# First attention of a two-block model kernel: reciprocal sums applied to the exponentials on GpSimd instead of to the head outputs

## The chip, the cores and the metric

One Trainium2 chip, one of its cores. The metric is the device time of one execution in microseconds (us). The engines named here: TensorE (PE) multiplies, PEld is its weight load; VectorE (DVE), ScalarE (ACT) and GpSimd (POOL) do the elementwise work; SyncE (SP) starts transfers. Each engine runs its own instructions in program order and waits on semaphores for the others.

## What is computed

The whole kernel is two transformer-like blocks of depth two, on 512 tokens of width 1024. The part that the change touches is the first attention (`mla_mix` in the first layer): twelve heads of 64, causal, 512 queries and 512 keys in blocks of 128.

```python
s = jnp.einsum('bhqd,bhkd->bhqk', qb, k) * scale
p = masked_softmax(s, key_pos[None, :] <= tq[:, None]).astype(v.dtype)
return jnp.einsum('bhqk,bhkd->bqhd', p, v)
# masked_softmax: e = exp(s - max) * mask;  e / max(sum(e), 1e-30)
```

After it come four heads of attention over 256 memory tokens (`memory_attention`), then the product with `w_out`, a layer norm, a feed-forward part, and so on.

## The kernel before

All work is written out by hand, engine by engine, and ordered by semaphores; nothing is scheduled by a tool. The twelve heads are the units u = 0 to 11 and are handled in six pairs i = 0 to 5. The four memory heads are the units 12 to 15. Two buffers of everything exist, and unit u uses buffer u % 2.

A unit goes through these steps, with the name of the helper and the engine:

1. `project_q` on TensorE: the query projection of one head, two matmuls of 512 columns into bank 3 of PSUM. `take_q` (ScalarE) and `rotate_q` (VectorE, three instructions) bring it to SBUF as QT.
2. `scores` on TensorE: four matmuls, one for each block of 128 queries, over 512, 384, 128 and 256 keys (the tiles in `STILES`), together 1280 columns.
3. `soft_max` on VectorE: adds the mask, takes the maximum, writes the masked scores to PR[:, s] in SBUF and the maximum to NB.
4. `softmax_exp` on ScalarE: the exponential in place in PR[:, s], and its row sums in SM[:, s]. It signals `p_ready`.
5. `own_sums` on VectorE: RS = 1/SM, 128x4. It signals `rs_ready`.
6. `probs_t` on TensorE: ten 128x128 transposes of PR[:, s]. `probs_out` on ScalarE and on VectorE copy the result to PT.
7. `pv_pair` (called by `mla_pv`) on TensorE: the product with the values for the two heads of a pair at once, transposed, so that features lie on the partitions and tokens on the columns.

The transposed probabilities are not normalised. `factors` on TensorE therefore multiplies the identity by RS spread over 64 columns, for both heads and four blocks of queries: eight small products that put 1/sum of every token on the 64 rows of each head. ScalarE copies the result to FR (`factors_out`, signal `factor_sb`), and VectorE multiplies the head outputs by it (`pair_out`, signal `o_done`).

TensorE's order inside `mla_pair(i)` is: transposes of unit 2i, projection of 2i+3, scores of 2i+2, transposes of 2i+1, scores of 2i+3, factors, projection of 2i+4, product with the values of pair i. The projection writes the same PSUM bank 3 as the factors before it, so it waits for `factor_sb`.

VectorE's order inside `mla_pair(i)` is: `pair_out` of pair i-1, `own_sums(2i)`, the copy of the transposes of 2i, `rotate_q(2i+3)`, `soft_max(2i+2)`, `own_sums(2i+1)`, the copy of the transposes of 2i+1, `soft_max(2i+3)`, `rotate_q(2i+4)`. Pair 4 has one projection only, and pair 5 none: the first two memory heads' scores stand in their place.

GpSimd has little in this stage: when ScalarE has rounded a chunk of the output to XH (`o_high`), it subtracts to get the rest, XL (`o_low`), one instruction of 128x512 for each of eight chunks. The memory heads keep the factors, before and after.

## Time and profile before

| | us |
|---|---|
| median of 3 runs | 2621.22 (2612.64 to 2634.3) |
| profiled execution | 2629.39 |
| its span | 2627.6 |
| PE busy in it | 2530.0 (96%) |
| DVE busy | 1454.3 (55%) |
| ACT busy | 961.7 (37%) |
| POOL busy | 1070.0 (41%) |
| first attention, twelve heads | from about 498 to 588 us of the span |

The busy figures count every instruction's duration. Matmuls overlap each other, and the gap between the starts of two groups tells more than a duration does. The clock granted to TensorE is 1.2 or 2.4 GHz and is printed as 0.50 or 1.00. In the page's 40 slices of the span it reads 9 tenths or more everywhere but in one slice, which reads 7.

### The profile page before, as it was taken

To read this page: it belongs to the slowest core of one execution; us is meant where nothing else is said; L and a number is where in the kernel's file an instruction comes from. 1 tells how busy PE (TensorE), PEld (TensorE's weight loads), DVE (VectorE), ACT (ScalarE), POOL (GpSimd) and SP (SyncE) were. 2 spreads that over 40 slices of the span, in tenths; PEclk is the share of its full clock that TensorE was granted. 3 is DMA by queue.
4 is the path that set the end of the run, shared out by engine and by line. 5 is a ranking of instruction groups with operands and counts; after the bars stand their busy time and mean duration, and the time that the engine had idled before them with its cause. 6 is when DMAs were issued, how large, how long until landed. Compare 5 with 4: busy or idle time off the path is not lost.

```text
span 2627.6 us, 34202 instructions
## 1 busy us (share of the span) xinstructions
PE 2530.0 (96%) x12558; PEld 2039.6 (78%) x12558; DVE 1454.3 (55%) x2060; ACT 961.7 (37%) x1500; POOL 1070.0 (41%) x712
## 2 busy tenths in 40 slices
PE   8999999899999999999999999889999998989998
PEld 7888887556788887888888777678888877777886
DVE  6545446664755646354654658564333354797653
ACT  4222225453522224232212578553222233353332
POOL 3978866003749834033633402273012054022401
PEclk9999999999999999799999999999999988999999
DMA  8354446211444463244442321235333235334231
GB/s 205 96 141 137 122 120 158 57 27 50 127 128 136 149 156 105 66 137 126 141 146 86 84 72 47 73 111 153 118 106 105 88 97 155 134 119 125 84 93 64
DMA packets 439113, 292.04 MB, mean 111 GB/s; under 512 B 34355, under 2 KB 420202, under 8 KB 435530
## 3 DMA queue, kind: packets, MB, share of 16 engines
q1 hardware_dynamic: 422042, 212.38, 28.6%
q0 software_dynamic: 16944, 77.93, 9.6%
q8 instruction: 83, 1.36, 0.2%
q14 instruction: 44, 0.36, 0.0%
HBM read 272.50 MB, written 20.92 MB: 112 GB/s over the span
## 4 chain that ended last, share of the span: by engine, by line
PE 83%; DVE 6%; POOL 5%; ACT 3%; issue 2%; DMA 1%; DVEq 0%; SPq 0%; ACTq 0%; POOLq 0%
PE ps L766 38%; PE ps L771 19%; PE ps L848 5%; PE ps L875 4%; PE ps L1055 2%; PE ps L1043 1%; DVE wl L2237 1%; POOL SW L3063 1%; POOL NS L3061 1%; PE ps L1458 1%; PE ps L1070 1%; PE ps L1416 1%; POOL NS L3060 1%; PE ps L1229 1%; PE ps L1195 1%
## 5 line engine op out<-in xcount | busy, mean ns | idle before, releaser
L2237 DVE TENSOR_TENSOR wl<-raw,wh 128x1024 fp32r<-128x1024 f32 x376 | 619.4, 1648 | 884.1 <-ACT wh L1681 880.9
L1681 ACT ACTIVATE wh<-raw 128x1024 fp32r<-128x1024 f32 x385 | 408.2, 1061 | 1329.4 <-PE ps L771 1160.4
L766 PE MATMUL ps<-XH,wh 128*128 128x512 f32 x1832 | 720.0, 393 | 0.5 <-ACT wh L1681 0.5
L766 PE MATMUL ps<-XL,wh 128*128 128x512 f32 x1832 | 713.9, 390 | 0.0
L771 PE MATMUL ps<-XH,wl 128*128 128x512 f32 x1832 | 453.2, 389 | 0.0
L766 PEld LDWEIGHTS ps<-XH,wh 128*128 128x128 f32 x1832 | 344.5, 188 | 77.1 <-issue 4.9
L766 PEld LDWEIGHTS ps<-XL,wh 128*128 128x128 f32 x1832 | 344.5, 188 | 73.1 <-issue 2.2
L771 PEld LDWEIGHTS ps<-XH,wl 128*128 128x128 f32 x1832 | 343.8, 188 | 71.7 <-issue 0.4
L766 PE MATMUL ps<-HH,wh 128*128 128x512 f32 x528 | 207.1, 392 | 0.0
L766 PE MATMUL ps<-HL,wh 128*128 128x512 f32 x528 | 205.5, 389 | 0.0
L3174 POOL TENSOR_TENSOR NS<-AW,CS 128x2048 f32<-128x2048 f32 x32 | 116.7, 3648 | 215.5 <-PE ps L1143 206.7
L771 PE MATMUL ps<-HH,wl 128*128 128x512 f32 x528 | 132.9, 391 | 0.9 <-DVE wl L2237 0.8
L771 PEld LDWEIGHTS ps<-HH,wl 128*128 128x128 f32 x528 | 98.9, 188 | 23.1 <-DVE wl L2237 2.0
L766 PEld LDWEIGHTS ps<-HL,wh 128*128 128x128 f32 x528 | 99.1, 188 | 21.5 <-issue 1.0
L766 PEld LDWEIGHTS ps<-HH,wh 128*128 128x128 f32 x528 | 99.1, 188 | 21.5 <-issue 1.0
L3011 POOL COPY ACC<-XT 128x512 f32<-128x512 f32 x6 | 3.7, 613 | 258.2 <-DVE XT L2302 258.2
L3175 POOL TENSOR_TENSOR NS<-NS 128x1024 f32<-128x1024 f32 x32 | 102.7, 3209 | 2.5
L3248 POOL DMA_DIRECT2D BS<-s_b x12 | 6.6, 559 | 227.3 <-PE ps L1195 181.3
L848 PE MATMUL ps<-XH,wh 128*128 128x512 f32 x172 | 77.5, 451 | 20.1 <-ACT XH L1766 10.3
L2257 DVE TENSOR_TENSOR HL<-HF,HH 128x512 f32 (+1 forms) x88 | 89.0, 1012 | 10.5
L1861 ACT ACTIVATE PR<-PR,NB 128x512 f32<-128x512 f32 (+3 forms) x144 | 79.0, 551 | 22.0 <-DVE NB L2520 21.3
L3155 POOL TENSOR_TENSOR XL<-O,XH 128x512 fp32r<-128x512 f32 x16 | 20.4, 1276 | 155.7 <-ACT XH L1894 155.7
(522 smaller groups left out, 4079.0 us busy)
## 6 DMA issues: line engine op xcount, KB each, us to landing
raw<-in_ffn_w_gu SPq DMA_DIRECT2D x176, 512.0 KB, 3.8
raw<-in_ffn_w_down SPq DMA_DIRECT2D x64, 512.0 KB, 3.7
AW<-in_ada_w POOLq DMA_DIRECT2D x24, 1024.0 KB, 7.5
raw<-in_ffn_w_down SPq DMA_DIRECT2D x32, 384.0 KB, 3.2
BS<-s_b POOLq DMA_DIRECT2D x12, 1024.0 KB, 6.1
raw<-in_odd_w_in SPq DMA_DIRECT2D x24, 512.0 KB, 3.8
raw<-in_even_w_in SPq DMA_DIRECT2D x22, 512.0 KB, 4.4
s_w<-SW POOLq DMA_DIRECT2D x12, 512.0 KB, 6.4
```

The lines of the kernel that those rows point to most:

```text
L766: pe.matmul(ps[:, p % 4, 0:n], wh[:, p % 2, k * P:(k + 1) * P], x[:, k, 0:n], start=k == 0 and x is hi, stop=False)
L771: mm = pe.matmul(ps[:, p % 4, 0:n], wl[:, p % 2, k * P:(k + 1) * P], hi[:, k, 0:n], start=False, stop=k == nk - 1)
L848: return pe.matmul(ps[:, (p + e) % 4, 0:n], w[:, (p + e) % 2, c * P:(c + 1) * P], x[:, c, 0:n], start=c == 0 and w is wh and x is hi, stop ...
L875: return pe.matmul(ps[:, (p + e) % 4, :], w[:, (p + e) % 2, k * P:(k + 1) * P], x[:, k, :], start=k == 0 and w is wh and x is HH, stop=k = ...
L1043: mm = pe.transpose(ps[:, bank, col:col + P], PR[:, s, POFF[q] + kb * P:POFF[q] + (kb + 1) * P], IDENT[:])
L1055: mm = pe.matmul(ps[e * HD:(e + 1) * HD, 7, kb * P:T], vals(kb, e), PT[:, e, at:at + T - kb * P], start=kb == 0, stop=kb == TT - 1)
L1681: act.activation(wh[:, p % 2, :], raw[:, p % 4, :], ACT.Copy).then_inc(w_hi, 1)
L1861: ins = act.activation(PR[:, s, POFF[t]:POFF[t] + (t + 1) * P], PR[:, s, POFF[t]:POFF[t] + (t + 1) * P], ACT.Exp, bias=NB[:, s, t:t + 1], ...
L2237: dve.tensor_tensor(wl[:, p % 2, :], raw[:, p % 4, :], wh[:, p % 2, :].bitcast(F32), ALU.subtract).then_inc(w_lo, 1)
L2257: dve.tensor_tensor(HL[:, k, :], HF[:, f:f + 1, :], HH[:, k, :].bitcast(F32), ALU.subtract).then_inc(h_ready, 1)
L3174: step(pool.tensor_tensor(prod, AW[:, n % 2], CS[:, :, e:e + 1].broadcast_to([P, KD, 2 * P]), ALU.mult))
L3175: step(pool.tensor_tensor(prod[:, 0:4], prod[:, 0:4], prod[:, 4:8], ALU.add))
```

## The change

Between the reciprocal and the transposes GpSimd now multiplies the exponentials in place by the reciprocal sums: `scale_probs`, four instructions for each of the twelve units, over 512, 384, 128 and 256 columns, with RS broadcast along the columns. The last of them signals `p_scaled`, and in the first layer `probs_t` waits for that in place of `p_ready`.

The factors of the six pairs go: `mla_factors` on TensorE, `factors_out` on ScalarE. `pair_out` becomes `plain_out` for them, a copy out of PSUM, at the same place in VectorE's order. `project_q` waits for `factor_sb` no more. `o_low` of chunk c stands behind the scaling of unit 2c+4 for c = 0 to 3. The counts of the later factors are lower by six (`PLAIN`), and the rotated key's semaphore is merged into `kv_ps`, which frees one semaphore.

```diff
@@ -423,7 +423,7 @@
         ln_aff = sem("ln_aff")
         mla_in_s = sem("mla_in_s")
         scaled = sem("scaled")
-        kr_ps = sem("kr_ps")
+        p_scaled = sem("p_scaled")
         kr_rot = sem("kr_rot")
         kr_keys = sem("kr_keys")
         x_read = sem("x_read")
...
@@ -570,6 +570,7 @@
 
             return 16 * (p // 4 + 1) + 32 * sum(q <= p and q % 4 == p % 4 for q in range(BASE["wo1"], BASE["wo1"] + COUNT["wo1"]))
 
+        PLAIN = HEADS // 2
         PAIR = {"mla": 0, "mem0": 6, "mem1": 8, "nsa": 10}
         S_WAIT = (1, 3, 3, 4)
         MEM_BANK = ((4, 2, 4, 2), (4, 6, 6, 4))
...
@@ -1036,7 +1037,10 @@
 
             def probs_t(u, s):
 
-                pe.wait_ge(p_ready, u + 1)
+                if mem_layer[0] == 0:
+                    pe.wait_ge(p_scaled, u + 1)
+                else:
+                    pe.wait_ge(p_ready, u + 1)
                 wait(pe, pt_act, 2 * u)
                 wait(pe, pt_dve, u)
                 for n, (bank, col, q, kb) in enumerate(TBLOCKS):
...
@@ -1107,7 +1111,7 @@
                                        start=m == 0, stop=m == MT - 1)
                 mm.then_inc(pv_ps, 1)
                 pe.wait_ge(rs_ready, u + 2)
-                pe.wait_ge(factor_sb, n)
+                wait(pe, factor_sb, n - PLAIN)
                 factors(MEM_PV[mem_layer[0]][h // 2][1], RS)
 
             def s5_fill(t):
...
@@ -1309,7 +1313,7 @@
                     pe.wait_ge(mla_in_s, 80)
                     pe.wait_ge(*taken_at("mla", 3))
                     pe.wait_ge(vm_ready, 4)
-                    pe.matmul(ps[ROPE:2 * ROPE, 6, :], PERM[:], KR, start=True, stop=True).then_inc(kr_ps, 1)
+                    pe.matmul(ps[ROPE:2 * ROPE, 6, :], PERM[:], KR, start=True, stop=True).then_inc(kv_ps, 1)
 
             panels("mla", 6, split_at("mla"), after=mla_squares)
             def project_q(h, s, turn):
...
@@ -1317,7 +1321,6 @@
                 pe.wait_ge(sp_in[s], 48 * turn + 48)
                 wait(pe, q_nope, h)
                 wait(pe, q_rot, 2 * h)
-                wait(pe, factor_sb, turn - 1)
                 for k in range(2):
                     mm = pe.matmul(ps[:, 3, :], WQ[:, s, k, :], CQ[:, k, :], start=k == 0, stop=k == 1)
                 mm.then_inc(q_ps, 1)
...
@@ -1363,17 +1366,9 @@
                 mla_scores(2 * i + 2, 0)
                 probs_t(2 * i + 1, 1)
                 mla_scores(2 * i + 3, 1)
-                mla_factors(i, 2 * i + 4)
                 if more > 1:
                     project_q(2 * i + 4, 0, i + 2)
                 mla_pv(i)
-
-            def mla_factors(i, projected, bank=3):
-
-                pe.wait_ge(rs_ready, 2 * i + 2)
-                pe.wait_ge(q_nope, projected)
-                pe.wait_ge(q_rot, 2 * projected)
-                factors(bank, RS)
 
             def mla_pv(i):
 
...
@@ -1385,7 +1380,6 @@
             probs_t(10, 0)
             mem_scores(12, 0)
             probs_t(11, 1)
-            mla_factors(5, 12, 6)
             mla_pv(5)
             mem_scores(13, 1)
             for h in range(MEM_HEADS):
...
@@ -1884,7 +1878,7 @@
 
             def factors_out(n, bank=3):
 
-                act.wait_ge(factor_ps, n + 1)
+                act.wait_ge(factor_ps, n + 1 - PLAIN)
                 wait(act, o_done, n)
                 act.activation(FR, ps[:, bank, :], ACT.Copy).then_inc(factor_sb, 1)
 
...
@@ -1949,7 +1943,7 @@
             take_q(0, 0)
             for g in range(14):
                 if g < 6:
-                    act.wait_ge(kv_ps, g + 1)
+                    act.wait_ge(kv_ps, g + 2)
                     act.activation(KT[0:HD, 2 * g, :], ps[0:HD, 4 + g % 4, :], ACT.Copy).then_inc(kv_act, 1)
                     if g == 5:
                         take_q(1, 1)
...
@@ -1957,7 +1951,7 @@
                         act.wait_ge(kr_rot, 2)
                         act.activation(KT[HD:QK, 0:6, :], KR2[:, 0:1, :].broadcast_to([ROPE, 6, T]), ACT.Copy).then_inc(kr_keys, 1)
                 elif g % 2 == 0:
-                    act.wait_ge(kv_ps, g + 1)
+                    act.wait_ge(kv_ps, g + 2)
                     act.activation(V[:, (g - 6) // 2, 0:6 * HD], ps[:, 4 + g % 4, 0:6 * HD], ACT.Copy).then_inc(kv_act, 1)
 
             take_q(2, 0)
...
@@ -1973,7 +1967,6 @@
                     take_q(2 * i + 3, 1)
                 softmax_exp(2 * i + 2, 0)
                 probs_out(2 * i + 1, 1)
-                factors_out(i)
                 softmax_exp(2 * i + 3, 1)
                 if more > 1:
                     take_q(2 * i + 4, 0)
...
@@ -1986,8 +1979,6 @@
                 probs_out(10 + h, h)
                 if h == 0:
                     o_high(4, (o_done, 5))
-                else:
-                    factors_out(5, 6)
                 mem_exp(12 + h, h, h)
             for h in range(MEM_HEADS):
                 u = 12 + h
...
@@ -2531,9 +2522,14 @@
 
             def pair_out(n, dst, bank=7):
 
-                dve.wait_ge(factor_sb, n + 1)
+                dve.wait_ge(factor_sb, n + 1 - PLAIN)
                 dve.wait_ge(pv_ps, n + 1)
                 dve.tensor_tensor(dst, ps[:, bank:bank + 1, :], FR.rearrange("p (o t) -> p o t", o=1), ALU.mult).then_inc(o_done, 1)
+
+            def plain_out(i):
+
+                dve.wait_ge(pv_ps, i + 1)
+                dve.tensor_copy(O[:, i, :], ps[:, 7, :]).then_inc(o_done, 1)
 
             def mem_max(u, n, s):
                 bank = MEM_BANK[n // 4][n % 4]
...
@@ -2619,7 +2615,7 @@
                 dve.tensor_tensor(QT[HD:QK, s, :], RT[HD:QK, 0, :], RT[HD:QK, 1, :], ALU.add).then_inc(q_rope, 1)
 
 
-            dve.wait_ge(kr_ps, 1)
+            dve.wait_ge(kv_ps, 1)
             dve.wait_ge(mla_in_s, 80)
             dve.tensor_tensor(KR2[:, 0, :], ps[ROPE:2 * ROPE, 6, :], ROT[ROPE:2 * ROPE, :], ALU.mult).then_inc(kr_rot, 1)
             dve.tensor_tensor(KR2[:, 1, :], KR, ROT[0:ROPE, :], ALU.mult).then_inc(dve_link, 1)
...
@@ -2628,14 +2624,14 @@
             rotate_q(0, 0)
             for g in range(14):
                 if g < 6:
-                    dve.wait_ge(kv_ps, g + 1)
+                    dve.wait_ge(kv_ps, g + 2)
                     dve.tensor_copy(KT[0:HD, 2 * g + 1, :], ps[HD:P, 4 + g % 4, :]).then_inc(kv_dve, 1)
                     if g == 5:
                         rotate_q(1, 1)
                         dve.wait_ge(kr_rot, 2)
                         dve.tensor_copy(KT[HD:QK, 6:12, :], KR2[:, 0:1, :].broadcast_to([ROPE, 6, T])).then_inc(kr_keys, 1)
                 elif g % 2:
-                    dve.wait_ge(kv_ps, g + 1)
+                    dve.wait_ge(kv_ps, g + 2)
                     dve.tensor_copy(V[:, (g - 6) // 2, 6 * HD:], ps[:, 4 + g % 4, 0:6 * HD]).then_inc(kv_dve, 1)
 
             def o_chunk(c):
...
@@ -2648,7 +2644,7 @@
             def mla_pair(i, more=2):
 
                 if not (isinstance(i, int) and i == 0):
-                    pair_out(i - 1, o_chunk(i - 1))
+                    plain_out(i - 1)
                 own_sums(2 * i, 0)
                 probs_out(2 * i, 0)
                 if more > 0:
...
@@ -2666,14 +2662,14 @@
             for h in range(2):
                 u = 10 + h
                 if h == 0:
-                    pair_out(4, o_chunk(4))
+                    plain_out(4)
                 own_sums(u, h)
                 probs_out(u, h)
                 mem_max(u + 2, h, h)
             for h in range(MEM_HEADS):
                 u = 12 + h
                 if h == 0:
-                    pair_out(5, o_chunk(5))
+                    plain_out(5)
                 if h == 2:
                     pair_out(6, o_chunk(6))
                 own_sums(u, u % 2)
...
@@ -3154,7 +3150,18 @@
                 pool.wait_ge(mix_hi, n + c + 1)
                 pool.tensor_tensor(XL[:, c, :], O[:, c, :], XH[:, c, :].bitcast(F32), ALU.subtract).then_inc(x_split, 1)
 
-            for c in range(KD):
+            def scale_probs(u, s):
+
+                pool.wait_ge(rs_ready, u + 1)
+                for t, bank, col in STILES:
+                    pr = PR[:, s, POFF[t]:POFF[t] + (t + 1) * P]
+                    ins = pool.tensor_tensor(pr, pr, RS[:, s, t:t + 1].broadcast_to([P, (t + 1) * P]), ALU.mult)
+                ins.then_inc(p_scaled, 1)
+            for u in range(HEADS):
+                scale_probs(u, u % 2)
+                if u >= 4 and u % 2 == 0:
+                    o_low(0, u // 2 - 2)
+            for c in range(HEADS // 2 - 2, KD):
                 o_low(0, c)
             norm("wo0")
 
```

The hunks left out only subtract `PLAIN` from a count of the memory heads and the second attention.

The order on TensorE in pair 1 of the twelve heads, before (PR are the exponentials, RS the reciprocal sums, CQ and WQ the query projection, KT and QT keys and queries, PT and V the transposed probabilities and the values):

```order
L1043 MATMUL ps<-IDENT,PR 128x128 [waits pt_dve,pt_act,p_ready]
L1043 MATMUL ps<-IDENT,PR 128x128 x9
L1070 MATMUL ps<-KT,QT 128x512 [waits s_sb,q_rope,q_nope]
L1070 MATMUL ps<-KT,QT 128x384 [waits s_sb]
L1070 MATMUL ps<-KT,QT 128x128 [waits s_sb]
L1070 MATMUL ps<-KT,QT 128x256 [waits s_sb]
L1062 MATMUL ps<-IDENT,RS 64x128 [waits q_rot,q_nope,rs_ready]
L1062 MATMUL ps<-IDENT,RS 64x128 x7
L1322 MATMUL ps<-CQ,WQ 128x512 [waits q_rot,factor_sb,q_nope,sp_in0]
L1322 MATMUL ps<-CQ,WQ 128x512
L1055 MATMUL ps<-PT,V 64x512 [waits o_done,pt_dve,pt_act]
```

and the same place of the change:

```order
L1047 MATMUL ps<-IDENT,PR 128x128 [waits pt_dve,pt_act,p_scaled]
L1047 MATMUL ps<-IDENT,PR 128x128 x9
L1074 MATMUL ps<-KT,QT 128x512 [waits s_sb,q_rope,q_nope]
L1074 MATMUL ps<-KT,QT 128x384 [waits s_sb]
L1074 MATMUL ps<-KT,QT 128x128 [waits s_sb]
L1074 MATMUL ps<-KT,QT 128x256 [waits s_sb]
L1325 MATMUL ps<-CQ,WQ 128x512 [waits q_rot,q_nope,sp_in0]
L1325 MATMUL ps<-CQ,WQ 128x512
L1059 MATMUL ps<-PT,V 64x512 [waits o_done,pt_dve,pt_act]
```

The eight products with RS are gone, the projection has lost the wait for `factor_sb`, and the transposes wait for `p_scaled`.

VectorE at the turn from one pair to the next, in the change (O is the head output, the copy stands where the multiplication by FR stood, so the order is that of before):

```order
L2610 TENSOR_TENSOR RT<-ps,ROT 32x512 [waits q_rope,q_ps]
L2611 TENSOR_TENSOR RT<-ps,ROT 32x512
L2615 TENSOR_TENSOR QT<-RT 32x512 [waits s_ps,q_rot]
L2532 COPY O<-ps 128x512 [waits pv_ps]
L2521 RECIPROCAL RS<-SM 128x4 [waits p_ready]
L2516 COPY PT<-ps 128x512 [waits t_ps]
```

The reciprocal of the first unit of a pair stays behind the copy that waits for the product of the pair before (`pv_ps`), and now the scaling and the transposes hang on that reciprocal.

GpSimd in the change, around the fifth unit:

```order
L3158 TENSOR_TENSOR PR<-PR,RS 128x512 [waits rs_ready]
L3158 TENSOR_TENSOR PR<-PR,RS 128x384
L3158 TENSOR_TENSOR PR<-PR,RS 128x128
L3158 TENSOR_TENSOR PR<-PR,RS 128x256
L3151 TENSOR_TENSOR XL<-O,XH 128x512 [waits mix_hi]
L3158 TENSOR_TENSOR PR<-PR,RS 128x512 [waits rs_ready]
```

Before, only the eight rows `XL<-O,XH` stood here.

## Rows read from the trace of the kernel before

**Rows 1.** The page's first part: busy time, share of span, instructions.
```profile
PE 2530.0 (96%) x12558; PEld 2039.6 (78%) x12558; DVE 1454.3 (55%) x2060; ACT 961.7 (37%) x1500; POOL 1070.0 (41%) x712
```
**Rows 2.** Busy time in a stretch; granted clock (PEclk), DMA share, GB/s last.
```profile
542.00:554.00 12.00, 11.21 (x72) 7.05 (x71) 8.41 (x27) 6.98 (x22) 0.00 (x0) 1.00 0.13 22
```
**Rows 3.** Timeline, TensorE in pair 2: start, us, engine, line, tiles, [idle before].
```profile
538.28 1.31 PE L1043 MATMUL ps<-IDENT,PR 128*128 128x128 f32 x10
541.15 2.32 PE L1070 MATMUL ps<-KT,QT 96*128 96x512 f32 x8
543.10 1.23 PEld L1043 LDWEIGHTS ps<-IDENT,PR 128*128 128x128 f32 x10
544.40 2.36 PE L1070 MATMUL ps<-KT,QT 96*128 96x512 f32 x8
546.69 1.09 PE L1062 MATMUL ps<-IDENT,RS 128*64 128x128 f32 x16
548.57 1.96 PE L1322 MATMUL ps<-CQ,WQ 128*128 128x512 f32 x4 [0.79 <-ACT NS L1889]
550.46 2.37 PE L1055 MATMUL ps<-PT,V 128*64 128x512 f32 x16
552.76 1.31 PE L1043 MATMUL ps<-IDENT,PR 128*128 128x128 f32 x10
```
**Rows 4.** Timeline, VectorE in the same pair 2.
```profile
538.47 0.69 DVE L2536 TENSOR_TENSOR O<-ps,NS 128x512 f32<-128x512 f32 x1 [0.25 <-PE ps L1055]
539.08 0.17 DVE L2530 RECIPROCAL RS<-SM 128x4 f32<-128x4 f32 x1
...
542.80 0.69 DVE L2619 TENSOR_TENSOR QT<-RT 32x512 f32<-32x512 f32 x1
...
543.52 0.69 DVE L2520 CUSTOM_DVE_ANT_0 PR<-ps,CAUS 128x512 f32<-128x512 f32 x1
...
545.16 0.17 DVE L2530 RECIPROCAL RS<-SM 128x4 f32<-128x4 f32 x1
```
**Rows 5.** GpSimd instructions by form: duration in ns min/median/max, first and last start.
```profile
L3174 POOL TENSOR_TENSOR NS<-AW,CS x32: 3603/3615/4652, 681.9 to 1390.3; 128x2048 f32<-128x2048 f32 x32
L3155 POOL TENSOR_TENSOR XL<-O,XH x16: 1262/1270/1296, 526.1 to 1684.2; 128x512 fp32r<-128x512 f32 x16
L3212 POOL TENSOR_TENSOR SC<-SC,CMASK x6: 727/736/739, 1574.9 to 1669.3; 128x256 f32<-128x256 f32 x6
```
**Rows 6.** Timeline, VectorE and GpSimd instructions that overlap, in a layer norm.
```profile
636.65 1.67 DVE L2237 TENSOR_TENSOR wl<-raw,wh 128x1024 fp32r<-128x1024 f32 x1 [0.47 <-ACT wh L1681]
637.20 2.28 POOL L3021 TENSOR_TENSOR NS<-NS 128x512 f32<-128x512 f32 x1
```
**Rows 7.** Timeline, first, fifth and last pair.
```profile
509.48 0.17 DVE L2530 RECIPROCAL RS<-SM 128x4 f32<-128x4 f32 x1
523.80 1.31 PE L1043 MATMUL ps<-IDENT,PR 128*128 128x128 f32 x10
567.24 1.31 PE L1043 MATMUL ps<-IDENT,PR 128*128 128x128 f32 x10
578.82 1.31 PE L1043 MATMUL ps<-IDENT,PR 128*128 128x128 f32 x10
581.98 1.07 PEld L1043 LDWEIGHTS ps<-IDENT,PR 128*128 128x128 f32 x10 [0.33 <-issue]
582.96 0.17 DVE L2530 RECIPROCAL RS<-SM 128x4 f32<-128x4 f32 x1
585.84 2.37 PE L1055 MATMUL ps<-PT,V 128*64 128x512 f32 x16 [1.52 <-ACT PT L1869]
588.14 1.99 PE L1086 MATMUL ps<-KM,QM 64*128 64x256 f32 x8
```
**Rows 8.** Two matmul groups behind idle stretches, and granted clock near the first.
```profile
505.47 3.62 PE L1070 MATMUL ps<-KT,QT 96*128 96x512 f32 x8 [3.05 <-DVE NB L2520]
507.00:508.00 1.00, 1.00 (x4) 0.70 (x3) 0.30 (x2) 1.00 (x5) 0.00 (x0) 0.50 0.00 0
```

More of the change, by code:

```diff
@@ L1082, in mem_scores @@
                 if h == 3 and layer == 1:
-                    pe.wait_ge(factor_sb, PAIR["mem1"] + 1)
+                    pe.wait_ge(factor_sb, PAIR["mem1"] + 1 - PLAIN)
                     pe.wait_ge(o_done, PAIR["mem1"] + 1)
@@ L1472, in nsa_factors @@
                 else:
-                    pe.wait_ge(factor_sb, PAIR["nsa"] + 2 * j + 1)
+                    pe.wait_ge(factor_sb, PAIR["nsa"] + 2 * j + 1 - PLAIN)
                 factors(bank, W4)
@@ L1483, in cmp_t @@
                 pe.wait_ge(c_p, j + 1)
-                pe.wait_ge(factor_sb, PAIR["nsa"] + 2 * j + 2)
+                pe.wait_ge(factor_sb, PAIR["nsa"] + 2 * j + 2 - PLAIN)
                 for t in range(TT):
@@ L1497, in _ @@
             pe.wait_ge(qs_ready, 2)
-            pe.wait_ge(factor_sb, PAIR["nsa"])
+            pe.wait_ge(factor_sb, PAIR["nsa"] - PLAIN)
             nsa_scores(20, 0, 0)
```

## Prediction

> **What bounds the kernel now.** I read the page's busy shares first: TensorE is busy 96% of the span and VectorE 55% [rows 1]. That is a mean over stages, so next the stretch of the first attention: in 12 us of pair 2 TensorE is busy 11.21 us at the full granted clock, GpSimd 0 us [rows 2]. The stage runs at TensorE's pace. The timeline then shows the cadence [rows 3]: the transposes of pair 2 start at 538.28, those of pair 3 at 552.76, so a pair takes 14.48 us, and each group starts where the one before ends, with one exception: the factors (L1062) start at 546.69 and the projection behind them only at 548.57, having waited for ScalarE's copy of the factors. These 1.88 us are factors plus wait. What the reader is to see besides is where the reciprocals stand [rows 4]. TensorE's transposes show no idle time before them, so the exponentials are there in time. But the reciprocals are late: the first of a pair runs at 539.08, after TensorE has begun the transposes of the same unit, and the second at 545.16, again after the transposes of its unit (543.10). Before the change nobody is hurt by that, since only the factors at 546.69 need them.
>
> **What the change removes.** The factors and the wait for their copy: 1.88 us in each of the pairs 0 to 3 [rows 3]. In pair 4 no projection follows, so only the products go, which I take as 0.9 (a duration of 1.09 that overlaps its neighbour). In pair 5 the factors lie under a wait: the product with the values waits another 1.52 us for ScalarE's copy of the transposes [rows 7]. ScalarE loses six copies, which are off the path. VectorE's multiplication becomes a copy of the same 128x512 from PSUM; I cost that at nothing; if it were 0.1 us off, six times that is below a microsecond.
>
> **What it adds: the price of one scaling, P.** Four GpSimd instructions over 512, 384, 128 and 256 columns. No row has just this form. From above: subtractions with two full inputs take 1.270 us for 512 and 0.736 us for 256 columns [rows 5], so 2.09 ns a column and 0.20 us fixed; that gives 1.27, 1.00, 0.47 and 0.74, together 3.48 us. From below: the multiplication by an operand broadcast along the columns takes 3.615 us for 2048 columns [rows 5], 1.77 ns each, which with nothing for four starts is 2.26 us for 1280. The operation is that of the second row, the sizes are those of the first. So I take 0.20 us for each start and (3.615 - 0.20)/2048 = 1.67 ns a column: 0.8 + 2.1 = 2.9, rounded to P = 3.0 us. The range keeps 2.26 and 3.48.
>
> **Where it lies.** Not beside anything. Take TensorE's first transposes of a pair in the old trace as T0 = 538.28.
> - First unit. VectorE's copy of the old pair's output stands ahead of the reciprocal and waits for TensorE's last product, so the reciprocal ends at 539.25, 0.97 us after T0 [rows 4]. GpSimd starts about 0.08 later, takes P, and TensorE hears of it about 0.09 later (hops like those between other engines here, an estimate). New start T1 = T0 + 0.97 + 0.17 + 3.0 = T0 + 4.14. Queued behind on TensorE: everything, in order.
> - Second unit. Its reciprocal stands behind the rotation and the soft_max of the next first unit, and these need the projection and scores that follow T1. In the old trace it ends at 545.33, T0 + 7.05: the rotation ends at 543.49, the soft_max starts at 543.52, and the reciprocal follows its last tile [rows 4]. All of it moves with T1. New start of the second transposes T2 = T1 + 7.05 + 0.17 + 3.0 = T1 + 10.22; in the old trace it was T0 + 4.82 (543.10).
> - From there TensorE runs through: 552.76 - 543.10 = 9.66 less 1.88 is 7.78 us [rows 3].
>
> A pair of the middle takes 4.14 + 10.22 + 7.78 = 22.14 us instead of 14.48: +7.66, three times +22.98. Pair 0: the first reciprocal ends at 509.65 [rows 7], transposes at 512.82, the next pair at 512.82 + 10.22 + 7.78 = 530.82 instead of 523.80: +7.02. Pair 4 takes 11.58 (567.24 to 578.82); its tail behind the second transposes is 11.58 - 4.82 - 0.9 = 5.86, so 4.14 + 10.22 + 5.86 = 20.22: +8.64. Pair 5: the second reciprocal ends at 583.13, 4.31 behind the first transposes (it has a memory head's maximum ahead of it instead of a soft_max); its transposes start 4.31 + 0.17 + 3.0 = 7.48 behind T1. The old tail 581.98 to 588.14 is 6.16, and less the 1.52 of waiting 4.64 [rows 7]. So 4.14 + 7.48 + 4.64 = 16.26 instead of 9.32: +6.94. **Sum: 7.02 + 22.98 + 8.64 + 6.94 = +45.6 us.** P is in it twelve times, so 2.26 gives +36.7 and 3.48 gives +51.4.
>
> `o_low` on GpSimd, moved into the stage, is 1.27 us behind a first unit's scaling [rows 5], while the second scaling comes 7.1 us after it: hidden. Were it not, it would cost at most 1.27 four times. Behind the stage TensorE goes straight on; no wait there could absorb the shift.
>
> **Does VectorE slow GpSimd down?** In the layer norm a GpSimd addition of 512 columns takes 2.28 us beside a VectorE subtraction that started first [rows 6], against 1.27 for a similar one alone. Here VectorE's instructions read PSUM, except the last of the rotation (0.69 us, ends at 543.49), and while GpSimd scales, VectorE waits for the very transposes that wait for GpSimd. So I add nothing. The Trainium skill (SBUF — State Buffer, the passage on the shared port pair) says that a VectorE instruction with two SBUF inputs contends with a GpSimd instruction that reads SBUF, and one with at most one doesn't. By that rule nothing is added either, and the slow row agrees with it. The skill's GPSIMD Engine Reference, section 4.1, advises against two-input elementwise work on GpSimd, about twice VectorE's time; by its 4497 ns for 2048 columns the scaling is an estimated 2.8 us, and the sum would be 2 us lower. The trace's subtractions are somewhat dearer.
>
> **What the stalls do to the clock.** TensorE will idle twice a pair, 4.1 us and 10.22 - 4.82 = 5.4 us, twelve stalls. Where it sat idle 3.05 us in the old trace, the scores behind took 3.62 us instead of 2.36, and the granted clock read 0.50, which is 1.2 of 2.4 GHz [rows 3, 8]. I expect that behind nearly every stall. If the first two groups behind a stall, some 3.3 us at the full clock [rows 3], go 3.62/2.36 = 1.53 times slower, a stall costs 1.7 us, and all of it is on the path, since these groups feed the next reciprocal or the next pair: 12 x 1.7 = +20 us. Ends: nothing, and 3 us a stall, +36. The Trainium skill (TensorE: Matmul & The Clock Gate, Part 1) says that idling drops the clock to half and sustained work restores it; the trace agrees, by the 0.50 behind the idle 3.05 us.
>
> **Total** 45.6 + 20 = +66 us. Against the profiled execution, 2629.4, that is 2695; it stands 8 us above the median of the runs, so by the median 2621.2 + 66 = **2687 us**, 2.5% slower.
>
> **The rivals.**
> - The clock stays up, or falls only now and then: +37 to +51, 2658 to 2673. For it: through a whole stage with TensorE 93% busy it holds. Against: the idle stretches are longer than the one that lost it. Chance 0.22.
> - The clock falls and stays low over most of the stage, or GpSimd takes 5 us a scaling (2.28 us for 512 columns as in [rows 6] would give 1280 x 4.45 ns = 5.7): +100 or more, above 2720. Against the first: dense groups follow every stall. Against the second: VectorE is waiting then. Chance 0.10.
> - The other side: the scaling is hidden and TensorE only loses the factors: 4 x 1.88 + 0.9 = -8.4 us, 2613. The mechanism would need the reciprocals one group of work earlier. They stand behind the previous product and behind the next soft_max [rows 4], and the order of VectorE is unchanged, so I give it 0.02. For the stage to cost under 1% (26 us), P would have to be below 3.0 - (45.6 - 26)/12 = 1.4 us even with the clock up, and no row of GpSimd is that fast: 0.03.
> - That the change doesn't do what it says is excluded by the order: `probs_t` waits for `p_scaled`.
>
> **How the numbers follow.** The forecast has 0.63. The range is from the clock staying up with the cheapest scaling, +37, less some scatter of the runs, to the dearest scaling with 3 us a stall, 51.4 + 36 = +87, plus scatter: 2655 to 2718. A difference under 1% can't be told from none here. Slower by over 1%: 0.63 + 0.22 + 0.10 = 0.95; within 1%: 0.04; faster: 0.01.
>
> **What the new profile would show.** Pairs of the stage 22 to 26 us apart instead of 14.48; before each group of transposes TensorE idle, released by GpSimd's PR; the four scalings together 2.3 to 3.5 us; the reciprocal 1 us behind the last product; the granted clock at 0.50 in parts of the stage; no wait for the copy of the factors. The sum is wrong if transposes start before the reciprocal's copy is done, if the scalings are much longer or shorter, or if time appears outside 508 to 600 us.

## The result and the profile after

The changed kernel takes 2684.98 us (median of 4 runs, 2677.88 to 2697.75) against 2618.08 us for the kernel before (4 runs, 2612.64 to 2634.3): 66.9 us more, a ratio of 1.0253 with a 95% interval of 1.0213 to 1.0292. The forecast was 2687 us. (The ratios and intervals of this document are estimated from all runs of a kernel and of the kernel before, and differ a little from the quotient of two medians.)

The page of the changed kernel, its busy time and two of its groups (line, engine, tiles, count | busy us, mean ns | idle before, and what ended it):

```profile
span 2696.0 us, 34023 instructions
PE 2552.4 (95%) x12462; PEld 2053.2 (76%) x12462; DVE 1457.8 (54%) x2060; ACT 960.7 (36%) x1494; POOL 1103.0 (41%) x760
L1047 PE MATMUL ps<-IDENT,PR 128*128 128x128 f32 x360 | 58.4, 321 | 51.4 <-POOL PR L3158 50.2
L3158 POOL TENSOR_TENSOR PR<-PR,RS 128x512 f32<-128x512 f32 (+3 forms) x48 | 33.0, 717 | 154.8 <-DVE RS L2521 154.8
```

The span has grown by 68.4 us. TensorE's busy time has grown by 22.4 of them (2552.4 against 2530.0 us, [rows 1]) although it executes 96 matmuls fewer, which already points at a lower clock; the other 46.0 are idle time. The third line tells where most of that lies: ahead of the transposes TensorE sat idle 50.2 us in all, released by GpSimd. GpSimd's 48 instructions are busy for 33.0 us, so the stalls are longer than the scaling itself.

TensorE's timeline over two pairs of the middle (start, us, engine, line, tiles, [idle before <- what ended it]):

```profile
539.20 2.40 PE L1047 MATMUL ps<-IDENT,PR 128*128 128x128 f32 x10 [3.83 <-POOL PR L3158]
541.39 3.36 PE L1325 MATMUL ps<-CQ,WQ 128*128 128x512 f32 x4
544.58 2.32 PE L1074 MATMUL ps<-KT,QT 96*128 96x512 f32 x8
551.65 2.39 PE L1047 MATMUL ps<-IDENT,PR 128*128 128x128 f32 x10 [4.75 <-POOL PR L3158]
553.84 2.70 PE L1074 MATMUL ps<-KT,QT 96*128 96x512 f32 x8
556.38 1.88 PE L1325 MATMUL ps<-CQ,WQ 128*128 128x512 f32 x4
558.19 2.38 PE L1059 MATMUL ps<-PT,V 128*64 128x512 f32 x16
564.40 2.02 PE L1047 MATMUL ps<-IDENT,PR 128*128 128x128 f32 x10 [3.83 <-POOL PR L3158]
...
590.22 2.39 PE L1047 MATMUL ps<-IDENT,PR 128*128 128x128 f32 x10 [3.83 <-POOL PR L3158]
```

These answer [rows 3]. Pairs start 25.2 and 25.8 us apart instead of 14.48. There is one stall ahead of each group of transposes, 3.83 us for the first unit and 4.75 us for the second, and behind each stall the transposes take 2.0 to 2.4 us, where they took 1.31.

VectorE and GpSimd in the same stretch, which answer [rows 4]:

```profile
548.60 0.17 DVE L2521 RECIPROCAL RS<-SM 128x4 f32<-128x4 f32 x1
548.85 2.75 POOL L3158 TENSOR_TENSOR PR<-PR,RS 128x512 f32<-128x512 f32 x4 [9.71 <-DVE RS L2521]
...
560.62 0.69 DVE L2532 COPY O<-ps 128x512 f32<-128x512 f32 x1 [0.18 <-PE ps L1059]
561.34 0.18 DVE L2521 RECIPROCAL RS<-SM 128x4 f32<-128x4 f32 x1
561.60 2.75 POOL L3158 TENSOR_TENSOR PR<-PR,RS 128x512 f32<-128x512 f32 x4 [9.99 <-DVE RS L2521]
564.31 1.26 POOL L3151 TENSOR_TENSOR XL<-O,XH 128x512 fp32r<-128x512 f32 x1
```

The chain is seen link by link: the product of the pair ends, VectorE copies it, takes the reciprocal, GpSimd scales for 2.75 us, TensorE transposes. GpSimd had been idle almost 10 us before each of these two scalings. The moved `o_low` (L3151) runs behind the scaling and delays nobody.

The windows of the changed kernel (behind the five busy times stand PEclk, the DMA share and GB/s), first from unit 1's scores to the first product with `w_out`, then about one pair:

```profile
506.00:681.00 175.00, 118.28 (x451) 72.13 (x452) 62.78 (x172) 59.11 (x177) 41.67 (x55) 0.77 0.05 12
542.00:567.00 25.00, 16.42 (x61) 9.67 (x60) 10.03 (x27) 8.39 (x25) 6.73 (x9) 0.84 0.06 11
```

The clock is 0.77 on average over the stage and 0.84 over that pair, where a stretch of the middle had 1.00 before [rows 2]. (The page of the kernel before has two slices of the clock at 8 besides the one at 7; all three lie behind this stage.)

For the experiments two lengths are read from each timeline: the heads' part, from the scores of unit 1 (505.47 in [rows 8]) to the product with the values of pair 5 (585.84 in [rows 7]), and the whole stage, on to the first product with `w_out`:

```profile
506.15 3.96 PE L1074 MATMUL ps<-KT,QT 96*128 96x512 f32 x8 [3.05 <-DVE NB L2511]
...
652.16 3.06 PE L1059 MATMUL ps<-PT,V 128*64 128x512 f32 x16 [0.47 <-ACT PT L1863]
...
681.21 0.50 PE L849 MATMUL ps<-XH,wh 128*128 128x512 f32 x1
```

In the changed kernel the heads' part is 652.16 - 506.15 = 146.01 us and the stage 175.06. Before, they were 80.37 and 107.03, by this line of the kernel before:

```profile
612.50 0.50 PE L848 MATMUL ps<-XH,wh 128*128 128x512 f32 x1
```

So the stage accounts for 68.0 of the span's 68.4 us, and the heads' part alone for 65.6. The other 2.4 lie in the memory heads, which take 29.05 us instead of 26.66 from the product of pair 5 to `w_out`, with slow groups in both. Each kernel's lengths come from one profiled execution.

| kernel | heads' part, us | stage, us | ratio of times to before, 95% |
|---|---|---|---|
| before | 80.37 | 107.03 | |
| changed | 146.01 | 175.06 | 1.0253 (1.0213 to 1.0292) |
| all reciprocals early | 78.92 | 108.63 | 1.0002 (0.9972 to 1.0032) |
| first reciprocal early | 120.72 | 148.69 | 1.0131 (1.0076 to 1.0187) |
| fillers of 7 and 8.6 us | 162.20 | 188.86 | 1.0286 (1.0231 to 1.0341) |
| fillers of 3.4 and 4.3 us | 122.76 | 150.96 | 1.0160 (1.0113 to 1.0206) |
| one tile scaled | 98.43 | 127.29 | 1.0066 (1.0028 to 1.0103) |
| no scaling | 73.45 | 106.72 | 0.9986 (0.9955 to 1.0017) |
| reciprocals early, memory heads filled | 75.10 | 98.89 | 0.9942 (0.9911 to 0.9972) |
| before, memory heads filled | 80.37 | 104.15 | 0.9978 (0.9943 to 1.0014) |

Outside the stage the ten profiled executions take 2501 to 2528 us, though no work was changed there. That the kernel before and the changed one agree there within 0.4 us is chance, and a gain of a few us is read from the stage and not from the whole.

### The profile page after: what moved, and what is told of

Read it like the earlier page. It is cut to its first block, busy times and chain, and to the rows that moved or that the text cites. A ratio compares the mean times of both kernels' runs of the same rounds, so it can differ in the third digit from the quotient of the medians.

```text
span 2696.0 us, 34023 instructions
## 1 busy us (share of the span) xinstructions
PE 2552.4 (95%) x12462; PEld 2053.2 (76%) x12462; DVE 1457.8 (54%) x2060; ACT 960.7 (36%) x1494; POOL 1103.0 (41%) x760
## 4 chain that ended last, share of the span: by engine, by line
PE 84%; POOL 6%; DVE 5%; ACT 3%; issue 1%; DMA 1%; SPq 0%; ACTq 0%; DVEq 0%; POOLq 0%
PE ps L767 37%; PE ps L772 19%; PE ps L849 5%; PE ps L876 4%; PE ps L1047 2%; PE ps L1059 2%; POOL SW L3059 1%; PE ps L1074 1%; POOL PR L3158 1%; DVE wl L2228 1%; POOL NS L3057 1%; PE ps L1452 1%; PE ps L1410 1%; POOL NS L3056 1%; PE ps L1325 1%
## 5 line engine op out<-in xcount | busy, mean ns | idle before, releaser
L1047 PE MATMUL ps<-IDENT,PR 128*128 128x128 f32 x360 | 58.4, 321 | 51.4 <-POOL PR L3158 50.2
L3158 POOL TENSOR_TENSOR PR<-PR,RS 128x512 f32<-128x512 f32 (+3 forms) x48 | 33.0, 717 | 154.8 <-DVE RS L2521 154.8
```

Source lines behind the costliest of these rows:

```text
L1047: mm = pe.transpose(ps[:, bank, col:col + P], PR[:, s, POFF[q] + kb * P:POFF[q] + (kb + 1) * P], IDENT[:])
L3158: ins = pool.tensor_tensor(pr, pr, RS[:, s, t:t + 1].broadcast_to([P, (t + 1) * P]), ALU.mult)
```

## The experiments

All edits are to the changed kernel unless it says otherwise.

### All reciprocals early

```diff
 rotate_q(2, 0)
 for h in range(2):
     soft_max(h, h, CAUS)
+for h in range(2):
+    own_sums(h, h)
 ...
     plain_out(i - 1)
-    own_sums(2 * i, 0)
     probs_out(2 * i, 0)
     if more > 0:
         rotate_q(2 * i + 3, 1)
     soft_max(2 * i + 2, 0, CAUS)
-    own_sums(2 * i + 1, 1)
     probs_out(2 * i + 1, 1)
     soft_max(2 * i + 3, 1, CAUS)
+    own_sums(2 * i + 2, 0)
     if more > 1:
         rotate_q(2 * i + 4, 0)
+    own_sums(2 * i + 3, 1)
 ...
 # pair 5
     if h == 0:
         plain_out(4)
-    own_sums(u, h)
     probs_out(u, h)
```

> The changed kernel with VectorE's reciprocals moved ahead: those of the next pair (units 2i+2 and 2i+3) are taken at the end of pair i, before VectorE waits for the product of pair i; nothing else differs. Theory A (the loss is the place of the reciprocals: scaling and transposes hang on reciprocals that stand behind the previous product and behind the next soft_max, 12 stalls, and the clock falls behind them): GpSimd scales one unit while TensorE works on others, TensorE waits for GpSimd nowhere in pairs 1 to 4 apart from some tenths of a us, a pair takes about 12.6 us (14.48 before, 25 in the changed kernel), the granted clock stays at 1.00 from the second pair on, the whole is about 2610 us, some 8 us below the kernel before. Theory B (GpSimd's 12 scalings of 2.75 us are a serial cost wherever the reciprocals stand, or they slow VectorE and ScalarE by contention): at least 12 x 2.75 = 33 us above the kernel before, 2650 or more, and TensorE still waits for PR.

Measured: 2619.04 us against 2620.27 for the kernel before, measured alongside, ratio 1.0002. TensorE ahead of the first transposes and in pairs 2 and 3:

```profile
515.39 2.40 PE L1047 MATMUL ps<-IDENT,PR 128*128 128x128 f32 x10 [3.44 <-POOL PR L3159]
...
542.89 1.31 PE L1047 MATMUL ps<-IDENT,PR 128*128 128x128 f32 x10
544.04 1.88 PE L1325 MATMUL ps<-CQ,WQ 128*128 128x512 f32 x4
545.75 2.32 PE L1074 MATMUL ps<-KT,QT 96*128 96x512 f32 x8
547.91 1.26 PE L1047 MATMUL ps<-IDENT,PR 128*128 128x128 f32 x10
...
555.32 1.31 PE L1047 MATMUL ps<-IDENT,PR 128*128 128x128 f32 x10
```

No wait for GpSimd is left in pairs 1 to 4 (in pair 5 there are 0.76 and 0.70 us), and a pair takes 555.32 - 542.89 = 12.43 us. GpSimd does the same 12 scalings of 2.75 us. So theory B falls: GpSimd's time is no cost by itself. Moving the reciprocals removes all of the 66 us. How they divide among the late reciprocals, GpSimd's time and the clock is read from the runs further below. But the whole did not drop below the kernel before, and 8 us of my expectation are missing. The heads' part is only 1.45 us shorter than before, since the first scaling still stalls TensorE 3.4 us, and the memory heads behind it take 3.0 us longer. The next experiment shows a loss at the same place without any scaling.

### No scaling at all

```diff
-                if mem_layer[0] == 0:
-                    pe.wait_ge(p_scaled, u + 1)
-                else:
-                    pe.wait_ge(p_ready, u + 1)
+                pe.wait_ge(p_ready, u + 1)
...
             for u in range(HEADS):
-                scale_probs(u, u % 2)
```

> The changed kernel without the scaling: GpSimd does not multiply, the transposes wait for the exponentials (p_ready) as before, so the head outputs stay unnormalised. It measures what the removal of the factors is worth alone. Theory A: 4 x 1.88 + 0.9 = 8.4 us below the kernel before, about 2610, pairs of 12.6 us, and the same as the kernel with early reciprocals within 2 us if the scaling is hidden there. Theory B (the factors were under other work, nothing to gain): the kernel before's time within 2 us, and the kernel with early reciprocals well above it.

Measured: 2621.37 us, ratio 0.9986. The interval of 0.9955 to 1.0017 shows no gain, but it doesn't exclude the 8.4 us that I had expected (0.9968) either. The timeline has both halves of an answer:

```profile
539.14 1.31 PE L1044 MATMUL ps<-IDENT,PR 128*128 128x128 f32 x10
...
551.57 1.31 PE L1044 MATMUL ps<-IDENT,PR 128*128 128x128 f32 x10
...
582.37 3.31 PE L1056 MATMUL ps<-PT,V 128*64 128x512 f32 x16 [2.54 <-ACT PT L1860]
585.62 3.78 PE L1087 MATMUL ps<-KM,QM 64*128 64x256 f32 x8
...
598.57 3.68 PE L1107 MATMUL ps<-PT,VM 128*64 128x512 f32 x8 [1.67 <-ACT PT L1874]
```

and its windows (PEclk third from the right):

```profile
509.00:583.00 74.00, 70.88 (x336) 43.16 (x338) 52.32 (x153) 46.47 (x142) 6.32 (x5) 0.96 0.13 27
583.00:604.00 21.00, 19.33 (x73) 11.82 (x67) 5.25 (x11) 5.47 (x21) 1.26 (x1) 0.52 0.01 1
```

The gain is there: pairs of 12.43 us, and the heads' part is 73.45 us, 6.9 less than before. A pair has gained 2.05 us where 1.88 was forecast. But pair 4 takes 575.36 - 564.00 = 11.36 us instead of 11.58, 0.2 less where 0.9 was forecast, because its product now waits 0.58 us for ScalarE. In this execution the gain is given back at once. With the factors gone from pair 5, TensorE waits 2.54 us for ScalarE instead of 1.52 [rows 7], and then it runs the memory heads at 1.2 GHz for 20 us (0.52 on average). Their scores take 3.78 us instead of 1.99. From the product of pair 5 to `w_out` it is 33.27 us where it was 26.66: 6.6 us lost. The size of this loss is that of one execution, the slowest of the kernel's twelve. Behind nearly the same wait (2.66 us) the kernel with all reciprocals early was back at the full clock sooner and took 29.71 us there. That the clock is the cause, and not ScalarE's pace, is tested below.

### Only the first unit's reciprocal early

```diff
+own_sums(0, 0)                     # behind the first two soft_max
 ...
     plain_out(i - 1)
-    own_sums(2 * i, 0)
     ...
     soft_max(2 * i + 3, 1, CAUS)
+    own_sums(2 * i + 2, 0)
 ...
 # pair 5
-    own_sums(u, h)
+    if h == 1:
+        own_sums(u, h)
```

> The changed kernel with only the reciprocal of each pair's first unit moved ahead of the wait for the product; the second unit's stays behind the next soft_max. Theory A: the stall of 3.8 us ahead of each first unit goes in pairs 1 to 5 (5 x 3.9 = 19.5), and with it the slow clock behind it (5 x about 1.6 = 8), together 28 us: about 2657; TensorE still waits 4.75 us ahead of each second unit. Theory B (GpSimd's serial time counts, not the place): no more than 5 us gained, 2680 or more.

Measured: 2657.07 us, as forecast. In the timeline of pairs 1 to 4 the first unit's transposes start without a wait, the second's with the same 4.75 us:

```profile
538.51 1.31 PE L1047 MATMUL ps<-IDENT,PR 128*128 128x128 f32 x10
...
548.45 2.40 PE L1047 MATMUL ps<-IDENT,PR 128*128 128x128 f32 x10 [4.75 <-POOL PR L3160]
```

The two stalls of a pair are separate, each with its own cause in VectorE's order. In pair 5 the first unit still waits 1.19 us. The heads' part is 25.3 us shorter than in the changed kernel, a little less than the 28 forecast, so the exact hit of the total is in part luck.

### Fillers in the stalls, too long

```diff
+FILL = (8, 10)
 def probs_t(u, s):
-    if mem_layer[0] == 0:
-        pe.wait_ge(p_scaled, u + 1)
-    else:
+    if mem_layer[0] != 0:
         pe.wait_ge(p_ready, u + 1)
     wait(pe, pt_act, 2 * u)
     wait(pe, pt_dve, u)
+    if mem_layer[0] == 0 and (isinstance(u, int) and u < HEADS):
+        for _ in range(FILL[u % 2]):
+            pe.matmul(ps[:, 0, :], IDENT[:], CQ[:, 0, :], start=True, stop=True)
+        pe.wait_ge(p_scaled, u + 1)
```

> The changed kernel with work put into TensorE's stalls: ahead of each of the 12 groups of transposes that wait for GpSimd, TensorE multiplies the identity by CQ into the transposes' bank, 8 times (first unit of a pair) or 10 times (second) with 512 columns, 0.43 us each at full clock, and waits for the scaling only then. The products are overwritten. Theory A (some 22 of the 66 us are the clock, which falls in the stalls): the fillers fit into the stalls of 3.8 and 4.75 us, the granted clock reads 1.00 through the stage, transposes take about 1.3 us again instead of 2.4, the whole drops by 18 to 25 us to about 2662. Theory C (the groups behind the stalls are longer for another cause, or the fillers don't hold the clock): 2685 or more.

Measured: 2700.58 us. The experiment was mis-sized and says nothing against theory A. One such instruction is two records of 0.43 us in the trace, so eight fillers lasted 7.0 us and ten 8.6, longer than the stalls:

```profile
564.91 7.13 PE L1048 MATMUL ps<-CQ,IDENT 128*128 128x512 f32 x16
571.88 1.25 PE L1051 MATMUL ps<-IDENT,PR 128*128 128x128 f32 x10
```

The second line already shows the transposes at 1.25 us again, and the granted clock reads 1.00 from 509 to 667 us.

### Fillers that fit

The same edit with `FILL = (4, 5)`.

> The changed kernel with the fillers again, 4 ahead of each first unit's transposes and 5 ahead of each second's: each filler is two matmul records of 0.43 us, so the 8 and 10 of before ran 7.0 and 8.6 us and overran the stalls; these take 3.4 and 4.3 us and fit. Theory A (the clock costs some 22 to 24 us of the changed kernel's 66): granted clock 1.00 through the stage, pairs of about 21.5 us instead of 25, the whole at about 2662 (2657 to 2667). Theory C (the transposes and what follows are slow for another cause than the clock): 2680 or more.

Measured: 2663.97 us, ratio 1.0160, and 1.0253 for the changed kernel.

```profile
559.79 1.31 PE L1051 MATMUL ps<-IDENT,PR 128*128 128x128 f32 x10 [0.20 <-POOL PR L3162]
...
581.07 1.31 PE L1051 MATMUL ps<-IDENT,PR 128*128 128x128 f32 x10 [0.21 <-POOL PR L3162]
```

```profile
538.00:560.00 22.00, 21.13 (x81) 10.78 (x81) 10.03 (x27) 8.21 (x23) 6.24 (x10) 1.00 0.07 13
```

The same order of work and the same scalings, with TensorE kept busy while it waits: the clock stays at 1.00 and a pair takes 21.28 us instead of 25.2 to 25.8. The heads' part falls from 146.01 to 122.76 us. So at least 23.3 us of it are the clock, and the remaining 122.76 - 80.37 = 42.4 us are the chain through VectorE and GpSimd with about 2 us of something else: ahead of the first and the last group the fillers still overran the scaling, by 0.8 and 0.4 us, and the scores of unit 1, where the heads' part begins, ran at the low clock for longer than before (4.61 us against 3.62). Theory C falls.

### One tile scaled

```diff
-                for t, bank, col in STILES:
+                for t, bank, col in STILES[2:3]:
```

> The changed kernel with GpSimd scaling only the tile of 128 columns of each unit and leaving the other 1152 columns unscaled: all waits and the order stay, P falls from 2.75 to about 0.45 us. Theory A: 12 x 2.3 = 28 us less from the stalls, and since the idle stretches shrink to some 1.5 and 2.5 us, most of the clock's 24 us too: 2630 to 2645, still 12 to 20 us above the kernel before, because of where the reciprocals stand. Theory D (the place of the reciprocals costs nothing, only GpSimd's time does): the kernel before's time or below, 2610 to 2620.

Measured: 2640.22 us, ratio 1.0066 to the kernel before. The scaling is down to one instruction of 0.40 us, and the stalls to 1.48 and 2.40 us:

```profile
538.38 2.21 PE L1047 MATMUL ps<-IDENT,PR 128*128 128x128 f32 x10 [2.40 <-POOL PR L3158]
...
549.03 1.31 PE L1047 MATMUL ps<-IDENT,PR 128*128 128x128 f32 x10 [1.48 <-POOL PR L3158]
...
556.62 1.31 PE L1047 MATMUL ps<-IDENT,PR 128*128 128x128 f32 x10 [2.40 <-POOL PR L3158]
...
565.60 1.31 PE L1047 MATMUL ps<-IDENT,PR 128*128 128x128 f32 x10 [1.48 <-POOL PR L3158]
```

With GpSimd nearly free the heads' part is still 98.43 us, 18 more than before. Theory D falls: these 18 us are the place of the reciprocals, twelve scalings of 0.40 us and what is left of the clock's losses.

The pair from 549.03 to 565.60 kept the clock and takes 16.57 us. With it the runs divide the changed kernel's pair into its parts. It is 12.43 us without the factors and with early reciprocals. Late reciprocals with 0.40 us of scaling make it 16.57, 4.1 more. The full scaling makes it 21.28, another 4.71, and that is twice the 2.35 us by which a scaling grows. The low clock makes it 25.2 to 25.8, another 3.9 to 4.5. So once the reciprocals are late, GpSimd's time counts in full, twice a pair. When they are early it counts for nothing.

### Reciprocals early, memory heads filled

The kernel with all reciprocals early, with two more edits: unit 0's reciprocal behind the first `soft_max`, and six fillers in TensorE's waits around the memory heads. The last group first waits for ScalarE's copy of the memory heads' first factors (`factor_sb`). The edit is shown against the kernel with all reciprocals early.

```diff
 for h in range(2):
     soft_max(h, h, CAUS)
-for h in range(2):
-    own_sums(h, h)
+    if h == 0:
+        own_sums(0, 0)
+own_sums(1, 1)
...
+def fill(count):
+    for _ in range(count):
+        pe.matmul(ps[:, 6, :], IDENT[:], CQ[:, 0, :], start=True, stop=True)
...
+fill(2)      # ahead of the product of pair 5
+fill(2)      # ahead of the first product of the memory heads
+fill(2)      # ahead of the transposes of memory head 3
```

> A version meant to beat both: the kernel with early reciprocals, unit 0's taken behind the first soft_max already, and TensorE's waits around the memory heads filled (two fillers ahead of the product of pair 5, two ahead of the first memory product, two ahead of the transposes of memory head 3). Theory E (the gain of 1.9 to 2 us a pair from dropping the factors is real, and it was given back behind the twelve heads, because TensorE there waits longer for ScalarE and ran 20 us at the low clock): from the scores of unit 1 to the first product of wo0 about 99 us instead of 107 before, the whole about 8 us below the kernel before, 2612. Theory F (ScalarE and VectorE bound the memory heads, the clock there is of no matter): the same time as the kernel before, 2620.

Measured: 2608.71 us against 2627.10 for the kernel before, measured alongside, ratio 0.9942 (0.9911 to 0.9972). It is faster than the kernel before, by 7 to 23 us. The stage takes 98.89 us, 8.1 less than before; 99 was expected. What the times show beyond these 8.1 us no changed work explains.

```profile
581.87 2.38 PE L1064 MATMUL ps<-PT,V 128*64 128x512 f32 x16 [0.95 <-ACT PT L1876]
584.17 1.99 PE L1095 MATMUL ps<-KM,QM 64*128 64x256 f32 x8
...
592.68 1.94 PE L1121 MATMUL ps<-PT,VM 128*64 128x512 f32 x8
...
605.66 0.50 PE L849 MATMUL ps<-XH,wh 128*128 128x512 f32 x1
```

```profile
507.00:606.00 99.00, 92.32 (x466) 55.29 (x465) 62.69 (x172) 56.41 (x178) 42.92 (x55) 0.98 0.10 21
```

The memory heads' scores take 1.99 us and their product 1.94, and from the product of pair 5 to `w_out` it is 23.79 us. With all reciprocals early and without fillers that was 29.71, without scaling 33.27, before 26.66. Filling idle stretches with products that nobody needs makes the groups behind them faster. So it was the low clock, and not ScalarE's or VectorE's pace, that took the gain back: theory F falls.

### The kernel before with fillers

Two of the three groups of fillers, ahead of the first memory product and of head 3's transposes, in the kernel before.

> The kernel before with two of these fillers groups alone (ahead of the first memory product and ahead of the transposes of memory head 3). Theory E: the low clock behind 605 us goes and with it 2 to 3 us, which the whole may not show (0.1%) but the timeline does: from the scores of unit 1 to the first product of wo0 104 to 105 us instead of 107. Theory F: 107 us or more.

Measured: 2613.12 us, ratio 0.9978 (0.9943 to 1.0014), which can't be told from none. The stage is 104.15 us instead of 107.03, as forecast:

```profile
506.83 3.43 PE L1075 MATMUL ps<-KT,QT 96*128 96x512 f32 x8 [3.05 <-DVE NB L2533]
...
610.98 0.50 PE L848 MATMUL ps<-XH,wh 128*128 128x512 f32 x1
```

From the product of pair 5 to `w_out` it is 23.78 us, the same as in the version above. Of the 8.1 us by which that version shortens the stage, 2.9 are thus to be had without the change, and 5.3, all in the heads' part, need it.

## Why the prediction was right, step by step

- **Place of the loss.** Right. All but 0.4 us of the longer span lies in the stage, TensorE waits for GpSimd 12 times. 2.4 us appear in the memory heads, which the sum had left at nothing.
- **The price P.** 3.0 us was taken, 2.75 measured. The working underneath was closer than the rounding: it had 0.20 us a start and 1.67 ns a column. The parts measured 0.40 us for 128 and 1.04 us for 512 columns, so 1.67 ns a column and 0.19 fixed, and neighbours overlap a little. I rounded 2.9 up. Twelve times 0.25 is 3.0 us too much.
- **The first unit's stall.** T0 + 4.14 was forecast. It is 3.89 with P = 2.75. In the new trace the copy starts at 560.62 and the transposes at 564.40; with the copy 0.19 behind T0, as in the old trace, that is 3.97. The reciprocal starts 0.72 us behind the copy, 0.61 behind the multiplication in [rows 4].
- **The second unit's stall.** 5.4 us was forecast with P = 3.0, 5.15 with 2.75, reckoned between starts. The row says 4.75 of idle time, and the scores' duration reaches 0.37 us past the start of what followed them in the old trace (541.15 + 2.32 against 543.10, [rows 3]).
- **The chain's sum.** +45.6 us, which is +42.6 with P = 2.75. Measured where the clock is kept up: +42.4 in the heads' part. That these agree within 0.2 us is luck, since the 42.4 hold some 2 us that are not the chain. A middle pair tells it more cleanly: 22.14 us were forecast, 21.64 with P = 2.75, and 21.28 measured. Of the remaining 0.36, 0.21 come from [rows 3], where I took the start of the weight load (543.10) for that of the second transposes (the trace has them at 543.31), and 0.17 from the factors, worth 2.05 us a pair and not 1.88.
- **The clock.** 1.7 us a stall and +20 us were forecast, 23.3 measured, 1.9 a stall. It fell at every one of the twelve stalls, as said: the transposes behind them take 1.97 to 2.40 us instead of 1.31. This term came out a little low and P a little high, and so the total is closer than its terms, by luck: 66 against 65.6 in the heads' part and 66.9 in the times. The rival in which the clock stays up had its price right too: with the fillers that fit, 2663.97 us, within its 2658 to 2673. The Trainium skill (TensorE: Matmul & The Clock Gate, Part 1) says that activity holds the full clock and idling loses it; the fillers agree with it, 1.00 over a pair against 0.84. That sustained work restores the clock, as the prediction quotes from there, isn't all: without scaling TensorE was busy for 12 us on end and the clock stayed at 0.50 (last section).
- **The rival on the other side.** Its condition was named rightly, reciprocals one group of work earlier: that is the first experiment, and there the scaling is hidden. Its price was not: -8.4 us counted TensorE's groups at the full clock up to `w_out`. Without scaling the trace shows 6.9 us gained in the heads' part and 6.6 lost behind it, through a longer wait for ScalarE and 20 us of low clock. I had written that the factors of pair 5 lie under a wait, and so put their removal at nothing. They were also what kept TensorE busy there: with fillers in that wait and in two others the loss is gone. No run has the filler of pair 5 alone, so its share isn't shown.
- **Contention.** Nothing was added, and twelve scalings of 2.75 us without a longer one show that nothing was to be added.

## What to carry to other kernels

When a step is put between two engines, look first at where in the producer's program its input is made, not at how long the step takes: here a scaling with 33 us of GpSimd work was hidden or came with a loss of 66 us, depending on where two reciprocals stand in VectorE's order. Of these 66 us no more than 33 were GpSimd's own. Ask of each idle stretch on TensorE what the groups behind it will cost at the lower clock, and price a removal of TensorE work in the same way: work that lies under a wait may be what holds the clock. A few matmuls on data at hand, shorter than the wait, are a cheap test for that, and may be worth keeping.

## What the runs showed of the hardware

- Equal stalls did not act alike. In the kernel with one tile scaled there are five of 2.40 us. Behind those at 538.38 and 573.19 the transposes took 2.21 and 2.40 us. Behind the one at 520.13 they took 1.31, but the scores after them 4.01 instead of 2.32. Behind those at 556.62 and 591.19 everything ran at the full clock. In the changed kernel, with stalls of 3.45 to 4.75 us, the clock was lost at all twelve.
- Being busy did not always bring the clock back. In the run without scaling, in the memory heads:

```profile
584.00:596.00 12.00, 12.00 (x39) 8.36 (x36) 4.47 (x10) 2.99 (x11) 1.26 (x1) 0.50 0.00 1
```

  TensorE is busy for all of these 12 us, and the granted clock stays at 0.50. In the kernel with all reciprocals early the same groups were at 1.00 again some 5 us behind the wait. No run shows what makes the difference.
- Where the scaling overlaps VectorE's work, the addition that ends the rotation is slowed. In the version with reciprocals early and the memory heads filled:

```profile
546.28 2.75 POOL L3173 TENSOR_TENSOR PR<-PR,RS 128x512 f32<-128x512 f32 x4 [5.28 <-DVE RS L2534]
...
548.58 1.00 DVE L2628 TENSOR_TENSOR QT<-RT 32x512 f32<-32x512 f32 x1
548.99 1.72 POOL L3166 TENSOR_TENSOR XL<-O,XH 128x512 fp32r<-128x512 f32 x1
```

  QT takes 1.00 us where it took 0.69 [rows 4], and XL 1.72 where it took 1.27 [rows 5]. Both sides read two tensors from SBUF. The copies and products of the rotation that read PSUM are not slowed. The Trainium skill (SBUF — State Buffer, the passage on the shared port pair) says that just such pairs contend; the trace agrees in kind, and the loss is some 0.3 to 0.45 us each. The instruction that was slowed is the one that started later: the scaling, already running when QT starts, still takes its 2.75 us.
- A GpSimd multiplication by an operand broadcast along the columns costs 1.67 ns a column and 0.19 us a start (from 0.40 us for 128 and 1.04 us for 512 columns). That is a fifth less a column than the 2.09 ns of the subtraction with two full inputs [rows 5].
